# Every activation placed 128 bytes over its weights, modulo 256: two small tiles moved, padding, wider rows for one operand

## The reference

```python
h = h + short_conv_mixer(rms_norm(h, a_norm), a_w_in, a_conv, a_w_out)
h = h + swiglu(rms_norm(h, f_norm[0]), f_w_gu[0], f_w_down[0])
h = h + nsa_mixer(rms_norm(h, b_norm), b_w_qg, b_w_o, *shared_kv(h, ...))
h = h + swiglu(rms_norm(h, f_norm[1]), f_w_gu[1], f_w_down[1])
x = rms_norm(h, final_norm)
x = x + gt_m * token_mixer(modulate(rms_norm_2(x, g_mix), sh_m, sc_m), w_in, ...)
x = x + gt_f * swiglu_2(modulate(rms_norm_2(x, g_ffn), sh_f, sc_f), w_gate, w_up, w_down)
```

## The kernel before

|---|---|---|---|
| opa with g | 160 | 224 | 64 |
| opb with g | 160 | 192 | 32 |
| hid with d | 192 | 224 | 32 |
| xin with g | 160 | 192 and 64, by turns | 32 and 160, by turns |
| dil (mixer's first half) with g | 160 | 192 | 32 |
| dil with mo2, mo3 (split ahead) | 32, 224 | 192 | 160, 224 |
| g with opa (line 1922) | 224 (opa is loaded) | 160 (g moves) | 192 |

## Time and profile before

### The profile page before, as it was taken

One profiled execution on the slowest core, in us unless ns is written; L12 is line 12 of the kernel. 1 busy time (PEld: TensorE's weight loads), 2 busy tenths in 40 slices (PEclk: granted clock), 3 DMA queues, 4 the chain that ended last, 5 costly groups with the idle time before them and its releaser, 6 DMA issues.

```text
span 956.1 us, 19360 instructions
## 1 busy us (share of the span) xinstructions
PE 940.2 (98%) x7852; PEld 906.8 (95%) x7852; DVE 711.9 (74%) x1135; ACT 489.8 (51%) x717; POOL 87.0 (9%) x132
## 2 busy tenths in 40 slices
PE   8999999999999999899999999999999999999998
PEld 8999999999999977599999999999998999999998
DVE  5896877777759978968777777698976767556554
ACT  6344744443447557846444444548667654443441
POOL 7000000000000042510000000030000000000000
PEclk9999999999999999999999999999999999999999
DMA  9756768686846742047686868335435447654611
GB/s 275 269 177 225 260 197 292 230 297 209 288 158 215 263 149 89 1 152 246 217 287 226 293 227 291 129 128 181 136 130 176 135 153 243 207 189 148 235 56 44
DMA packets 129851, 186.97 MB, mean 196 GB/s; under 512 B 6400, under 2 KB 100992, under 8 KB 129792
## 3 DMA queue, kind: packets, MB, share of 16 engines
q1 hardware_dynamic: 122016, 159.69, 50.4%
q0 software_dynamic: 6912, 25.17, 7.4%
q10 hardware_dynamic: 864, 1.29, 0.4%
HBM read 185.09 MB, written 1.05 MB: 195 GB/s over the span
## 4 chain that ended last, share of the span: by engine, by line
PE 87%; DMA 4%; DVE 3%; ACT 3%; SPq 1%; issue 1%; DVEq 0%; ACTq 0%
PE ps L1924 45%; PE ps L2002 19%; PE ps L1920 12%; PE ps L1922 4%; DMA g_raw<-in_a_w_in 2%; ACT g_hi L694 1%; DMA g_raw<-in_w_up 1%; DMA w_v<-in_cmp_w_v 1%; PE ps L2131 1%; PE ps L2078 1%; PE ps L2196 1%; PE ps L2211 1%; DVE g_lo L1201 1%; ACT opb_hi L712 0%; ACT e_odd L908 0%
## 5 line engine op out<-in xcount | busy, mean ns | idle before, releaser
L1924 PE MATMUL ps<-opa_hi,g_hi 128*128 128x256 f32 x864 | 224.6, 282 | 2.1 <-ACT g_hi L811 0.7
L1924 PE MATMUL ps<-opa_lo,g_hi 128*128 128x256 f32 x864 | 216.9, 279 | 0.0
L1924 PE MATMUL ps<-opa_hi,g_lo 128*128 128x256 f32 x864 | 178.2, 279 | 0.0
L1319 DVE TENSOR_TENSOR g_lo<-g_raw,g_hi 128x2048 fp32r<-128x2048 f32 x54 | 123.8, 2293 | 69.1 <-ACT g_hi L768 69.1
L1924 PEld LDWEIGHTS ps<-opa_hi,g_hi 128*128 128x128 f32 x864 | 162.2, 188 | 5.8 <-issue 3.5
L1924 PEld LDWEIGHTS ps<-opa_lo,g_hi 128*128 128x128 f32 x864 | 158.9, 188 | 0.1
L2002 PE MATMUL ps<-hid_hi,d_hi 128*128 128x256 f32 x528 | 148.0, 280 | 0.0
L2002 PE MATMUL ps<-hid_hi,d_lo 128*128 128x256 f32 x528 | 147.6, 280 | 0.0
L2002 PE MATMUL ps<-hid_lo,d_hi 128*128 128x256 f32 x528 | 147.2, 279 | 0.0
L1201 DVE TENSOR_TENSOR g_lo<-g_raw,g_hi 128x2048 fp32r<-128x2048 f32 x54 | 123.6, 2290 | 26.5 <-ACT g_hi L694 23.1
L1924 PEld LDWEIGHTS ps<-opa_hi,g_lo 128*128 128x128 f32 x864 | 135.4, 187 | 0.0
(11 more groups left out here) (345 smaller groups left out, 1805.2 us busy)
## 6 DMA issues: line engine op xcount, KB each, us to landing
g_raw<-in_f_w_gu SPq DMA_DIRECT2D x44, 1024.0 KB, 8.9
ada_raw<-in_w_ada POOLq DMA_DIRECT2D x48, 512.0 KB, 6.7
d_raw<-in_f_w_down SPq DMA_DIRECT2D x22, 1024.0 KB, 5.1
g_raw<-in_w_in SPq DMA_DIRECT2D x14, 1024.0 KB, 8.3
g_raw<-in_w_gate SPq DMA_DIRECT2D x11, 1024.0 KB, 7.5
g_raw<-in_w_up SPq DMA_DIRECT2D x11, 1024.0 KB, 9.8
d_raw<-in_w_down SPq DMA_DIRECT2D x11, 1024.0 KB, 5.3
g_raw<-in_a_w_in SPq DMA_DIRECT2D x8, 1024.0 KB, 7.5
```

The costliest lines, as they stand in the source:

```text
L1319: dve.tensor_tensor(part_view(g_lo, g0 + r, True), raw_cols(c % 2, r % 2, True), part_view(g_hi, g0 + r, True).bitcast(F32), ALU.subtract) ...
L1924: mm = pe.matmul(pair(b)[:, a, :], wt[:, a * P:(a + 1) * P], xt, **st)
```

## The change

nmax and zsum (64 bytes each) move from behind gates to the place of pad_x_res (64 bytes), so all that follows starts 64 bytes later: xres, opa, ybuf, gu, hid, rstd and the small constants. csil, any_vis and if_bias lose their own tiles: csil becomes the c_2 columns of par, in place, and the other two become columns 3 to 5 of eps. Behind them addresses fall by up to 160 bytes. Paddings before mo2, before d_raw and in the shared region grow by 32 or 128 bytes, and a row of xin grows from 288 to 320 columns. No instruction is added, removed or put elsewhere, and no wait is changed.

```diff
-    sb("pad_x_res", [P, 2 * HALF_LINE])
+    nmax = sb("nmax", [P, 2, 8])
+    zsum = sb("zsum", [P, 2, 8])
     xres = sb("xres", [P, KT, T])
...
-    eps = sb("eps", [P, 3])
+    eps = sb("eps", [P, 6])
     par = sb("par", [P, NROWS])
-    csil = sb("csil", [P, KT])
...
-    if_bias = sb("if_bias", [36, 1])
     gates = sb("gates", [P, TT, 48])
-    nmax = sb("nmax", [P, 2, 8])
-    zsum = sb("zsum", [P, 2, 8])
...
-    any_vis = sb("any_vis", [P, TT])
...
-    sb("pad_mo2", [P, 3 * HALF_LINE], on=over)
+    sb("pad_mo2", [P, 4 * HALF_LINE], on=over)
...
-    xin_hi = sb("xin_hi", [P, KT, T + 32], F32R, on=over)
-    xin_lo = sb("xin_lo", [P, KT, T + 32], F32R, on=over)
+    xin_hi = sb("xin_hi", [P, KT, T + 64], F32R, on=over)
+    xin_lo = sb("xin_lo", [P, KT, T + 64], F32R, on=over)
...
+    sb("pad_d", [P, 4 * HALF_LINE], on=over_b)
     d_raw = sb("d_raw", [P, 2, 2, D], on=over_b)
...
-    sb("pad_b", [P, 4096], on=over_b)
+    sb("pad_b", [P, 4096 + 4 * HALF_LINE], on=over_b)
...
-    sb("over_b_extent", [P, 12288])
+    sb("over_b_extent", [P, 12288 + 4 * HALF_LINE])
...
+    csil = par_col("c_2", 0, 8)
+    any_vis = eps[:, 3:5]
+    if_bias = eps[0:36, 5:6]
...
-        act.activation(csil[:, :], par_col("c_2", 0, 8), ACT.Silu).then_inc(csil_made, 1)
+        act.activation(csil, csil, ACT.Silu).then_inc(csil_made, 1)
```

## The result

The changed kernel takes 966.85 us (median of 5 runs, 966.05 to 968.65) against 953.38 us for the kernel before on the same chip (5 runs, 951.65 to 958.19). The ratio is 1.0121, 95% interval 1.0093 to 1.0149: it is slower, and the prediction, 928.5 us, has the wrong sign. The measured time lies above its whole range. Of the cases named, the slower rival came nearest: every matmul further apart, and 966.85 us just above its 959 to 966.

The account below looks back on a forecast made before the run. TensorE was taken as the bound, through the distance between matmuls. 20.3 us saved in the SwiGLUs (7.0, 5.3, 8.0) plus 3.1 outside made 23.4 off 951.97, so 928.5 us; 8-in-10 range 921 to 958.

Parts of the forecast that it names:

- the slower rival: All stages: at 128 loads meet the moving stream more often, 119 to 120 ns a matmul; +7 to +14 us, 962; chance 0.18.
- What bounds the kernel, and by what it could move: Whole kernel: TensorE, busy 98% of the span, sets the end; only the distance between matmuls can move the time.
- I take the fast pace (113.4 ns): Wide and down steps at offset 128: 113.4 ns a matmul, a round 8.16 us, 20.3 us saved in the SwiGLUs.
- 64, 128 and 192 are alike in that activation and weights start at the same place modulo 64.: First reason for 113.4 ns at 128: every fast step is of this kind, none at 32 or 160 is.
- A fast pattern once found isn't broken at the border of a step.: Second reason for 113.4 ns: one offset for wide and down steps ends the first SwiGLU's alternation of 64 and 32.
- the fast steps all lie outside the SwiGLUs: Kernel before: 113.3 to 113.8 ns seen only in the mixer's input projection and the sparse attention's output projection.
- the two more columns of xin: Third SwiGLU's wide steps: 258 columns at 114.2 ns a matmul against 113.4, taken as 256/258.
- the runs' median is 6.0 lower than the profiled execution: Base of the forecast: profiled execution 957.94 us, runs' median 951.97, from which 23.4 us was taken.
- Fast in part: Rival: fast pace found by chance, held in one or two of three SwiGLUs; 5 to 15 us less, 941; chance 0.17.
- No change: Rival: offset isn't the cause, or 128 has the 117.9 ns pattern; xin gains 1.6 us; about 952.5 us; chance 0.20.
- Costs taken as zero: Moved small tiles and silu of c: zero, within 0.5 us; new DMA targets: zero, remote worst case 26 us.
- The rule weighed: Against the forecast: moving data and weights use independent SBUF ports, so addresses cannot matter and the time stays.

Follow-up runs that it names:

- s64: Changed kernel with weights and activations both moved 64 bytes on, offset left at 128; 967.19 us, ratio 1.0099 to the kernel before.
- w64: Changed kernel with only the weights moved 64 bytes on, so that the offset is 64; 957.87 us, ratio 1.0004 to the kernel before.
- a192: Changed kernel with activations moved 64 bytes on, offset 192 (64 in the mixer's token steps); 955.14 us, ratio 0.9981 to the kernel before.
- b192: a192 with xin, the third SwiGLU's wide-step operand, at offset 16; 947.73 us, ratio 0.9905 to the kernel before.
- h64x256: Changed kernel loading only 64 weight columns in the first SwiGLU's wide steps and streaming 256 columns, not 258, in the third's; 962.22 us, one execution.
- w0: Changed kernel with the weights moved 128 bytes on, offset 0; 972.75 us, ratio 1.0159 to the kernel before.
- f16: Changed kernel with weights 16 bytes off the 32-byte grid, differing from f48 in the pads alone (offsets 16, 176, 80, 240); 962.17 us, one execution.
- o32: Kernel before with opa moved back 32 bytes and xin rows 320 columns apart, main offsets all 32; 957.08 us, ratio 0.9996.
- b32: o32 with xin, the third SwiGLU's wide-step operand, at offset 16; 955.86 us, ratio 0.9999 to the kernel before.
- a224: Changed kernel with activations moved 96 bytes on, offset 224 (32 in token steps); 964.25 us in one execution, beside 956.75 for the kernel before.
- f48: Changed kernel with weights 16 bytes off the 32-byte grid (offsets 48, 80, 208); 958.70 us in one execution, beside 957.35 for the kernel before.
- a96: Changed kernel with weights 64 and activations 32 bytes on, offset 96 (160 in token steps); 973.13 us, ratio 1.0196 to the kernel before.

## Why the prediction was wrong

**What bounds the kernel, and by what it could move: right.** Same number of matmuls, same clock, same work on the other engines, and the difference in the distance of matmuls.

**"I take the fast pace (113.4 ns)": this step failed.** 128 has 118.7 ns in every SwiGLU of the changed kernel and of s64, 120.0 ns in a few other steps, and never the fast pace. Both reasons fell:

- "64, 128 and 192 are alike in that activation and weights start at the same place modulo 64." 64 and 192 are alike (w64, a192). 0 and 128, of the same kind, have 120.0 and 118.7 ns. The likeness was read off the fast steps alone; every fast step before was at 64 or 192, and that was all the rows said.
- "A fast pattern once found isn't broken at the border of a step." It often isn't (b192 holds it over many borders), but at one offset throughout a border did break it: in b192 at the first down step of the first and of the second SwiGLU, without an interruption. An interruption can end it too (b192 at 472 us, a192 after 120.90 us) or bring it back (b192 at 120.44 us), and the slow pattern is as lasting. w64 had one offset throughout and no SwiGLU at 113.3 ns. Nor did "the fast steps all lie outside the SwiGLUs" hold: in the kernel before, the first wide step of the first SwiGLU, at 112.91 us, has 113 to 114 ns between its starts after a first gap of 0.19 us, which its piece of 5.68 us hides.

The sum also gave the two more columns of xin 0.8 ns (114.2 against 113.4; 258/256 of 113.4 is 114.3). At 128 they cost 3.2 ns (121.9 against 118.7, h64x256), so xin got slower than at its old offsets.

The map from the runs, streamed over loaded operand, 256 columns, ns a matmul:

| offset | pace | from |
|---|---|---|
| 0 | 120.0 | w0 |
| 16 | 120.0 or 117.5 | f16 (SwiGLU; a mixer step) |
| 32 | 116.7 | o32, b32, a224's token steps |
| 48 | 116.9 | f48 |
| 64 | 117.7 or 113.3 | w64, a192's token steps |
| 80 | 118.1 | f48 |
| 96 | 120.0 | a96 |
| 128 | 118.7, in a few steps 120.0 | the changed kernel, s64 |
| 160 | 118.8 or 117.3 | a96's token steps |
| 176 | 119.0 | f16 |
| 192 | 117.7 or 113.3 | a192, b192, w64's token steps |
| 208 | 117.9 or 119.2 | f48's down steps; its token steps |
| 224 | 118.3 | a224, o32's token steps |
| 240 | 117.1 | f16's token steps |

**The slower rival** had the path, matmuls further apart, and nearly the pace (119 to 120 ns); its reason, that the loads meet the moving stream more often, is not shown. Its sums for the SwiGLUs are a little high: first +1.7 to 3.3 us forecast and 1.4 measured, second 3.6 to 5.2 and 3.0. For xin it had -0.4 to +0.6; measured are (5.85 - 5.77) x 21 = 1.7 us. Its whole, +7 to +14 us, takes in the 9.3 us by which the profiled executions differ (967.25 - 957.94). That its 962 us still fell short of 966.85 comes from the base, 951.97 us, the median of three executions, of which the prediction itself noted that "the runs' median is 6.0 lower than the profiled execution". In the later comparisons 52 executions of the kernel before have a median of 956.9 us. 966.85 is 10.0 above that, near the 9.3 of the profiles, while the medians of the result differ by 13.5: its five executions of the kernel before were probably, by luck, among the better ones, and the loss is nearer 1.0% than 1.2% (s64, of the same pace, has a ratio of 1.0099).

The spreads point to why the kernel before has better executions. Executions of kernels with one main pace lie close together: w0 within 1.8 us, s64 1.6, o32 1.8, b32 2.8, the changed kernel 2.6, and a96 5.5 (its longest at a mean granted clock of 0.995). Those with 64 or 192 in them spread: w64 over 10.6, a192 12.3, b192 8.8, and the kernel before in its runs 951.32 to 964.11. The clock makes a part of this, but at 0.999 or 1.000 the kernel before still spreads over 7.0 us, w64 over 9.5 and o32 over 1.5. One SwiGLU at 113.3 instead of 117.7 ns is worth (8.48 - 8.16) x 22 = 7.0 us, so the spread is of the size of one or two of them. That the executions differ by this is inferred from one profiled execution of each kernel and the times of the others.

**"Fast in part"** described the kernel before, and b192, but not 128. **"No change"** took xin to gain 1.6 us when its offset no longer turns; it lost 1.7. Only the turn itself went, as said.

**Costs taken as zero** were so, to what the profile tells: d_raw landed in 5.1 against 5.0 us, ScalarE waited 85.8 against 84.8 us for VectorE's product, VectorE was busy 712.2 against 711.9 us. s64 and w64, with other DMA targets again, follow the offset alone.

**The rule weighed**, the Trainium skill, "TensorE: Matmul & The Clock Gate", Part 2 (What happens when you issue a matmul), has the streamed data and the weights read through two independent ports. The prediction drew from it that addresses cannot matter. For these fp32r matmuls the runs disagree with that: when the weights are moved and the activations stay, the pace goes from 118.7 to 117.7 (w64) and 120.0 ns (w0).

**Open:** which of the two paces a start at 64 or 192 takes, why 96 is as slow as 0, why 128 and 160 have a second pace in a few steps, and what holds a matmul at 116.7 ns when half of the weights and of the outputs are left out. The runs give the paces, not the mechanism behind them.

## What to carry to other kernels

Where TensorE bounds and matmuls of one shape show several paces, give each candidate layout a run of its own before reasoning from likeness: here offsets 32 bytes apart differed by 3.3 ns a matmul (0 and 32), and the likenesses that were assumed beforehand (64, 128 and 192; an offset and its mirror; the mean of the neighbours) failed, but for that of 64 and 192. Look at the spread of the executions as well as at one profile: a kernel that is sometimes fast may have two patterns, and a median of a few of its executions contains luck (953.38 us over five here, 956.9 over 52 later ones). And place the operands of other widths (the 258 columns here) apart from the rest, since their best offset is another.

## What the runs showed of the hardware that was not expected

- Matmuls of 128 x 128 fp32r weights on 256 columns, at granted clock 1.00 and with weights loading beside them, start every 113.3 to 120.0 ns, by the byte offset of the streamed over the loaded operand modulo 256 (table above); with weights 16 bytes off the grid of 32, the same offset had 117.9 and 119.2 ns in two kinds of step (208, f48). hid over d stands 128 bytes modulo 256 but 384 modulo 512 in the changed kernel, opa over g 128 modulo both, and both have 118.7 ns, so here offsets that are 256 apart are alike.
- At 64 and 192 there are two lasting patterns, 113.3 and 117.7 ns; the change from one to the other stood at a gap in some places (two starts 0.22 us apart in b192, 0.58 us in a192) and in others at the border of two steps without one (the first down steps in b192).
- Two columns more, 258 for 256, cost 3.2 ns at offset 128 (121.9 against 118.7), and at 16 the 258 columns go at 116.9 and 117.9 ns by turns where 256 columns in the same kernel took 120.0 in the first SwiGLU (f16).
- Loading 64 weight columns instead of 128 at offset 128, and so making half of the outputs, shortens the distance by 2.0 ns, from 118.7 to 116.7.
